# Squares by halves at one stage entrance, a later branch on TensorE, and warm-up products

## The reference

```python
# first block, each layer l
x = x + mixer(rms_norm(x, ...))            # l = 0: pooling, l = 1: latent attention
x = x + hier_moe(rms_norm(x, ffn_norm[l]), ...)   # 32 experts, 2 per token
# between the blocks
x = rms_norm(x, final_norm)
# second block, each layer l
h = swiglu(_rmsnorm(x, g[0]), w_in[l, 0], w_out[l, 0])   # stage "ffn00" for l = 0
x = x + 0.5 * _rmsnorm(h, g[1])
...
```

## Time and profile before

| | us |
|---|---|
| median of 3 runs | 2067.85 (2067.81 to 2069.82) |
| profiled execution | 2067.81 |
| its span, from the first to the last instruction | 2066.0 |
| TensorE busy | 1941.6 (94%) |
| VectorE, ScalarE, GpSimd busy | 877.4, 671.9, 60.4 |
| HBM read | 595.86 MB, 289 GB/s over the span |

### The profile page before, as it was taken

One profiled execution on the slowest core, in us unless ns is written; L12 is line 12 of the kernel. 1 busy time (PEld: TensorE's weight loads), 2 busy tenths in 40 slices (PEclk: granted clock), 3 DMA queues, 4 the chain that ended last, 5 costly groups with the idle time before them and its releaser, 6 DMA issues. The chain is left out here.

```text
span 2066.0 us, 36371 instructions
## 1 busy us (share of the span) xinstructions
PE 1941.6 (94%) x16078; PEld 1376.6 (67%) x16078; DVE 877.4 (42%) x1393; ACT 671.9 (33%) x1138; POOL 60.4 (3%) x97
## 2 busy tenths in 40 slices
PE   6999888988999999999989999999999999999998
PEld 6444344445875444444458888878888888887887
DVE  4011111104651111111156656876665665786663
ACT  2000000003440000000054546664545554676552
POOL 0000000000000000000020000010000000011000
PEclk8999999999999999999999999999999999999999
DMA  9999999998769999999976555336555555425551
GB/s 386 426 426 427 426 427 425 428 424 358 268 244 402 426 428 426 427 425 427 425 288 222 187 180 184 123 116 231 186 181 191 203 190 184 147 100 192 192 195 62
DMA packets 57340, 599.42 MB, mean 290 GB/s; under 512 B 6608, under 2 KB 7120, under 8 KB 10320
## 3 DMA queue, kind: packets, MB, share of 16 engines
q1 hardware_dynamic: 56016, 593.52, 71.9%
q10 hardware_dynamic: 1152, 3.41, 0.6%
HBM read 595.86 MB, written 1.05 MB: 289 GB/s over the span
## 5 line engine op out<-in xcount | busy, mean ns | idle before, releaser
L1972 DVE TENSOR_TENSOR SPLIT<-RING,SPLIT 128x2048 fp32r<-128x2048 f32 (+2 forms) x178 | 398.8, 2256 | 143.1 <-ACT SPLIT L1450 142.8
L752 PE MATMUL PS<-RING,WK 128*32 128x512 f32 x816 | 368.0, 605 | 45.6 <-DVE WK L2236 23.6
L1119 PE MATMUL PS<-HTB,SPLIT 128*128 128x512 f32 x1152 | 404.4, 397 | 0.0
L1450 ACT ACTIVATE SPLIT<-RING 128x2048 fp32r<-128x2048 f32 (+2 forms) x178 | 332.7, 1887 | 47.0 <-DMA RING<-in_units 47.0
L1120 PE MATMUL PS<-HTB,SPLIT 128*128 128x256 f32 x1152 | 321.4, 279 | 0.0
L752 PEld LDWEIGHTS PS<-RING,WK 128*32 128x32 f32 x816 | 86.9, 111 | 289.2 <-issue 253.2
L1119 PEld LDWEIGHTS PS<-HTB,SPLIT 128*128 128x128 f32 x1152 | 216.3, 188 | 51.7
L1598 ACT ACTIVATE WK<-PS 128x128 f32<-128x128 f32 x64 | 17.8, 278 | 700.4 <-PE PS L718 695.7
L1120 PEld LDWEIGHTS PS<-HTB,SPLIT 128*128 128x128 f32 x1152 | 217.0, 188 | 0.2
L718 PE MATMUL PS<-RING,WK 128*32 128x128 f32 x5696 | 184.4, 274 | 7.0 <-issue 5.7
L718 PEld LDWEIGHTS PS<-RING,WK 128*32 128x32 f32 x5696 | 160.3, 109 | 31.0 <-issue 27.3
(11 more groups left out here) (335 smaller groups left out, 2328.3 us busy)
## 6 DMA issues: line engine op xcount, KB each, us to landing
RING<-in_units SPq DMA_DIRECT2D x171, 1024.0 KB, 4.8
RING<-in_w_down SPq DMA_DIRECT2D x53, 2048.0 KB, 35.2
RING<-in_w_gate SPq DMA_DIRECT2D x45, 2048.0 KB, 34.4
RING<-in_w_up SPq DMA_DIRECT2D x44, 2048.0 KB, 36.5
WK<-in_w_up SPq DMA_DIRECT2D x17, 2048.0 KB, 37.8
WK<-in_w_gate SPq DMA_DIRECT2D x16, 2048.0 KB, 36.0
WK<-in_w_down SPq DMA_DIRECT2D x6, 2048.0 KB, 35.2
SEAT<-in_w_up SPq DMA_DIRECT2D x3, 2048.0 KB, 27.8
```

Source lines behind the costliest of these rows:

```text
L752: t = pe.matmul(PS[32 * i:32 * i + 32, 4 + h, :], mo.HE[:, pb, 32 * f:32 * f + 32], v[:, c, 512 * h:512 * h + 512], start=f == 0, stop=f == 3)
L1119: pe.matmul(out.rearrange("p (z b n) -> p z b n", z=2, b=2), wh, HTB[:, :, :, c, :], start=start, stop=False)
L1450: ac.activation(unit_part(u, 0), loaded(u), ACT.Copy).then_inc(s_hi, 1)
L1972: dv.tensor_tensor(unit_part(u, 1), loaded(u), unit_part(u, 0).bitcast(F32), ALU.subtract).then_inc(s_lo, 1)
```

## The change

1. **Squares by halves at the entrance to `ffn00`.** ScalarE squares a half row of 512 columns at a time, of `X` as well as of the gained row, and GpSimd adds up four partial sums instead of two. VectorE makes the gained row in two halves, each with its own semaphore count.
2. **Order at the entrance.** On VectorE the gained row of block 1 moves from ahead of `enter` to behind the low half of u0+1. On ScalarE the high half of u0+1 moves from behind the squares of block 0 to behind the eight `halves` of block 0.
3. **TensorE's branch.** In `moe0` it moves from ahead of step 27 to ahead of step 31. In `moe1` it moves behind step 32 and the last combine, and only the overflow path is left in it, so nothing is written twice there.
4. **Warm-up products.** In both expert layers three go ahead of the `up` products of expert 31, and three behind its turn, ahead of the down products of expert 30.

```diff
-            if n in (2,) or n >= 5:
-                return (4 if n == 2 else 12 + 4 * (n - 5)) + 2 * b + h + 1
-            return {0: 0, 1: 2, 3: 8, 4: 10}[n] + b + 1
+            if n == 2 or n >= 4:
+                return (4 if n == 2 else 10 + 4 * (n - 4)) + 2 * b + h + 1
+            return {0: 0, 1: 2, 3: 8}[n] + b + 1
...
                 part = SM[:, 8 + b:9 + b]
+                po.wait_ge(s_sq, squared(4, b, 0))
+                po.tensor_scalar(part, SM[:, b:b + 1], EPS, EPS * EPS, ALU.mult, ALU.add).then_inc(own.up(), 1)
                 po.wait_ge(s_sq, squared(4, b))
-                po.tensor_scalar(part, SM[:, b:b + 1], EPS / 1024, EPS * EPS, ALU.mult, ALU.add).then_inc(own.up(), 1)
-                po.wait_ge(s_fsq, b + 1)
                 po.wait_ge(own.sem, own.n)
-                po.tensor_tensor(part, part, SM[:, 10 + b:11 + b], ALU.add).then_inc(own.up(), 1)
+                po.tensor_scalar(part, SM[:, 24 + b:25 + b], EPS, part, ALU.mult, ALU.add).then_inc(own.up(), 1)
+                po.wait_ge(s_fsq, 2 * b + 2)
+                po.wait_ge(own.sem, own.n)
+                po.tensor_scalar(part, SM[:, 10 + b:11 + b], SM[:, 14 + b:15 + b], part, ALU.add, ALU.add).then_inc(own.up(), 1)
...
                 for z, name in enumerate(("gate", "up")):
+                    if z and e == 31:
+
+                        keep_warm(pe, 2, 3)
                     pe.wait_ge(*landed((name, l, e)))
...
                         turn_hidden(e)
+                        keep_warm(pe, 2, 3)
                     down(e - 1)
...
-            early = 27
+            early = 31 if l == 0 else 33
 
             def end():
                 for e in range(early, 33):
                     step(e)
-                combine(7)
+                if l == 0:
+                    combine(7)
             for e in range(early):
...
+            if l:
+                combine(7)
             with pe.If(over > 0):
                 end()
                 pe_overflow(pe, l)
-            with pe.Else():
-                end()
+            if l == 0:
+                with pe.Else():
+                    end()
...
                 def gained(b):
-                    ac.wait_ge(s_fg, b + 1)
-                    square(XS[:, b, :], SM[:, 10 + b:11 + b], (s_fsq, b + 1), scale=1 / 32)
+                    for h in range(2):
+                        ac.wait_ge(s_fg, 2 * b + h + 1)
+                        square(XS[:, b, 512 * h:512 * h + 512], SM[:, 10 + 4 * h + b:11 + 4 * h + b], (s_fsq, 2 * b + h + 1),
+                               JK[:, 512 * h:512 * h + 512], 1 / 32)
...
                 gained(0)
-                hi(u0 + 1)
                 scale(0)
                 squares(n, 1)
                 halves(stage, 0)
+                hi(u0 + 1)
                 gained(1)
...
                 lo(u0 + 1)
+                gained(1)
                 scale(1)
...
-                    if l:
-                        gained(1)
...
-                dv.tensor_tensor(XS[:, b, :], X[:, b, :], RB[:, 2, :], ALU.mult).then_inc(s_fg, 1)
+                for h in range(2):
+                    c = 512 * h
+                    dv.tensor_tensor(XS[:, b, c:c + 512], X[:, b, c:c + 512], RB[:, 2, c:c + 512], ALU.mult).then_inc(s_fg, 1)
```

More of the change, by code:

```diff
@@ L568, in pool_program @@
             for b in range(2):
-                inverse_rms(SM[:, 12 + b:13 + b], SM[:, b:b + 1], 1024, (s_sq, squared(4, b)), 1.0, s_frs)
+                inverse_rms_of_halves(SM[:, 12 + b:13 + b], (SM[:, b:b + 1], SM[:, 24 + b:25 + b]), 1.0, (s_sq, squared(4, b)),
+                                      s_frs)
             po.wait_ge(s_x, 8)
@@ L1462, in squares @@
             def squares(n, b):
-                if n in (0, 1, 3, 4):
+                if n in (0, 1, 3):
                     x_ready(n, b)
@@ L1470, in squares @@
                     else:
-                        ac.wait_ge(*((s_cx, 29 + b) if n == 2 else (s_xh, 2 * (n - 5) + b + 1)))
+                        ac.wait_ge(*((s_cx, (29 if n == 2 else 59) + b) if n in (2, 4) else (s_xh, 2 * (n - 5) + b + 1)))
                     square(X[:, b, 512 * h:512 * h + 512], SM[:, b + 24 * h:b + 24 * h + 1],
@@ L2038, in scale @@
                 def scale(b):
-                    dv.wait_ge(s_fg, b + 1)
+                    dv.wait_ge(s_fg, 2 * b + 2)
                     dv.wait_ge(s_rs, 2 * n + b + 1)
```

## The result

The changed kernel took 2080.76 us (median of 4 runs, 2076.13 to 2082.2) beside 2068.84 us of the kernel before (4 runs, 2067.81 to 2070.18): ratio 1.0054, 95% interval 1.0042 to 1.0066, so about 11 us slower. All 21 runs of it on record lie between 2076.1 and 2084.5, with a median of 2080.3. The direction was forecast, the size not: 2080.8 lies outside the range of 2069.3 to 2076.3. The profiled execution took 2079.38 us, with a span of 2077.5.

The account below looks back on a forecast made before the run. With TensorE busy 94% of the span, only its idle stretches, at the expert layers' ends and the handover, could matter. Terms 0 + 0 + 4.8 + 0.6 = +5.4 us on about 2067.8 gave 2073.3 us, range 2069.3 to 2076.3.

Parts of the forecast that it names:

- The bound of the stretches: Last weight slabs decide both expert layers' ends; in the handover to `ffn00` TensorE waits for the vector side.
- one for wrong: Sign against the forecast: u0+2 starts before 1074 us, or a stretch outside the handover moves by over 1.5 us.
- Part 1: Warm-up products at expert 31, both layers: slab waits and ScalarE cover them, 0; 1.2 us lost without layer 1's cover.
- Part 2: TensorE's moved branch: fetch gaps hidden, 0; up to 1.3 us in layer 0, at most 0.5 in layer 1.
- the rule alone: Taken branch forces a fetch; 1.0 us sticks out behind layer 1's combine, giving 2074.3 us; set aside as hidden.
- the rows on who is awaited: Trace rows at the handover where TensorE waits for the vector side; taken to hide the branch's fetch, so 0.
- Part 3: Entrance to `ffn00`: moved squares and high half delay u0+1 by 1.6 us and u0+2 by +4.8 us, the term.
- the clock: Handover: idle ahead of u0+2 may drop TensorE to 1.2 GHz, 4 in 10; +0.6 us, ends 0 and 1.7.
- (a): Rival, slower: layer 0's fetch gap (1.3) and the clock fall (1.7) come on top; 2075.7 us, chance 0.12.
- (b): Rival, no change: ScalarE and VectorE catch up at the handover, +0.9 to +4, about 2070.5 us; chance 0.24.
- (c): Rival, faster: expert layer ends decide, last down quarters no longer wait for DMA; -4.9, 2063 us; chance 0.06.

Follow-up runs that it names:

- e2: Kernel before with only the warm-up trios at expert 31 of both layers; 2068.5 us, ratio 0.9998.
- e14: Kernel before with TensorE's branch moved in layer 0 only, plus both trios in both layers; 2075.5 us, ratio 1.0022.
- e16: Changed kernel without any warm-up trios; 2075.4 us, ratio 1.0028.
- e18: Changed kernel with the warm-up trios in layer 1 only; 2076.7 us, ratio 1.0036.
- e1: Kernel before with only TensorE's branch moved, in both layers; 2071.0 us, ratio 1.0014.
- e11: Changed kernel with TensorE's branch left out in both layers; 2074.5 us, ratio 1.0023.
- e4: Kernel before with TensorE's branch moved in layer 0 only; 2071.4 us, ratio 1.0008.
- e13: Changed kernel without the trio ahead of `up` 31, the trio behind the turn kept; 2080.8 us, ratio 1.0058.
- e15: Kernel before with TensorE's branch moved in layer 1 only, plus both trios in both layers; 2072.6 us, ratio 1.0010.
- e9: Kernel before with the changed entrance and TensorE's branch moved in layer 1 only; 2075.3 us, ratio 1.0028.
- e5: Kernel before with TensorE's branch moved in layer 1 only; 2071.4 us, ratio 1.0011.
- e8: Kernel before with the branch moved in both layers and the trios, entrance as before; 2077.7 us, ratio 1.0037.
- e3: Kernel before with only the entrance changed (squares by halves, new order on ScalarE and VectorE); 2074.2 us, ratio 1.0028.
- e10: e3 with the gained row of block 1 back ahead of the entrance on VectorE; 2069.8 us, ratio 1.0007.
- e17: Changed kernel with only the trio ahead of `up` 31, in both layers; 2076.3 us, ratio 1.0031.
- e12: Kernel before with trios, whole-row squares and another entrance order, block 1's gained row behind the low half of u0+2; 2067.3 us, ratio 0.9985.
- e6: Changed kernel with TensorE's branches where they were before (new entrance and trios only); 2074.5 us, ratio 1.0028.

## Why the prediction was wrong in size

**The bound of the stretches.** Right for the kernel before, and the reason of the error. "At both ends of the expert layers the last slab of weights decides" was used as if it were fixed. The slack it leaves in layer 0 was 1.16 and 0.36 us, plus 1.14 us at 490.96, ahead of the down products, that the text did not count: 2.7 us together. The two gaps of the changed kernel (1.62 and 3.23 us) and its two trios (4.2) come to 9.1, so 6.4 would stick out by this estimate; 5.7 did. Of the signs that the text gave, one for wrong came true, a stretch outside the handover that moves by over 1.5 us.

**Part 1, warm-up products: 0.** Right by themselves (e2). The text named the cover of the first trio, the wait of 1.16 us for the slab of `up` 31, and priced its loss at 1.2 us. It did not ask whether Part 2 takes that cover away. It does: both trios lie on the path in layer 0, the first one at half clock in the profiled execution, behind the gap, and cost some 4 to 5 us there (e14, e16, e18).

**Part 2, the branch: 0, at most 1.3 in layer 0.** This is the step that failed. Both moved branches cost 2.1 us alone (e1, interval 1.0 to 4.8), and 6 to 7 us together with the trios (e11 against the changed kernel). Four things were off. The gap was 3.23 us, not 2.54 (2.06 to 3.64 in the kernels that have it). Of 2.54 us the text let 1.3 reach the end; with the waits that it names it is 1.0, and with the 1.14 us it left out nothing, which is what e16 shows for a single gap of 2.77. A second gap by issue, of 1.62 us (up to 2.17 in others), now falls 14 us ahead of it in seven of the ten profiled executions with this branch (e4, e13 and e16 lack it), where in the kernel before the last gap, at 430 us, left 67 us to catch up with the slabs. The estimate stopped at the gap: in six of these ten the granted clock is at 0.50 right behind it, and what stands next runs at half speed. And in layer 1 the overlap was wrong. The text let the fetch begin at about 1054.4, with the combine, and end 4.7 us behind the combine's start. In all eleven kernels with that branch the packet of q8 starts only 3.8 to 4.0 us behind it (in e13 and e15 the first of two at 3.6 and 3.4), and TensorE restarts at 6.3 to 6.6 us, in e13 and e15 at 7.9 and 7.8. The Trainium skill (Runtime: NRT & Kernel Launch, Instruction fetch mechanics) says that a taken branch outside what is held forces a fetch; the trace agrees (2.67 to 2.88 us of "issue" behind the last combine with a packet of q8 in it, gone in e11). By the rule alone I had 2074.3, and gave it away to the rows on who is awaited. In the handover the rows on who is awaited were right all the same when the clock held (e1, e9: handover as without the branch, because u0+1 is awaited longer) and wrong when it fell (e5, +1.8 us; e8, +3.2).

**Part 3, the entrance: +4.8, and the clock: +0.6.** Right in its mechanism and, within a microsecond, in its size. Alone it measured +5.3 us (e3), and what decides is what the text named, the gained row of block 1 and its squares ahead of the high half of u0+2 (e10). By the traces u0+2 starts 4.05 us later in e3 and 3.5 in e11 (21.06 less 17.57), so the term was mis-sized by about 1 us: u0+1 came 1.2 us later, not 1.6, and the gained row in halves took 1.29 us, not 1.4. GpSimd's power took 0.56 us as taken, and the scale came 0.2 us sooner behind the combine, as forecast (0.25). A unit takes 3.0 us by the text's own rows (3.5 less 0.46), not 2.7, so its idle time ahead of u0+2 would be 3.6 us and not 3.9; nothing hangs on it. The clock was worth more where it fell: in e3, in its slowest execution, u0+2 runs its first eight products cold, some 1.6 us, against the 0.6 that I counted as a mean; in e11 it did not fall on u0+1 or u0+2.

**The rivals.** (a), the gap and the clock on top of the entrance, was the nearest, with half the size: it added 1.3 and 1.7 us, 3.0 in all, where the changed kernel took 6.5 more than e11. It had no trios in it, and they are the larger part. (b) is what e10 shows, a milder entrance; it was not this kernel. (c) did not happen: the last quarter of the down products no longer waits for a DMA in layer 0, as its condition says, but because TensorE is late and not because the slabs came early.

**What stays open.** e13 and e17 together: the trio behind the turn costs 4.5 us by the times (changed kernel 2080.8, e17 2076.3), the other one nothing (e13, 2080.8). By the rows it should be 1.4 and 2.8. The ratios of e13 (1.0045 to 1.0072) and e17 (1.0020 to 1.0042) don't overlap, so the scatter of the runs hardly explains it. Leaving a trio out also moves the place of the gap (in e17 it opens inside the trio, and the clock holds), and no run separates the two; it isn't settled. Nor is it known what decides, in a given execution, whether the clock falls behind the gap.

## What to carry to other kernels

A price of 0 that rests on a wait holds only as long as no other part of the same change uses that wait up: add the parts that share one cover and compare the sum with it. An instruction fetch that falls early in a stretch paced by DMA is made up for; moved to the end of the stretch, the same fetch can be paid, and what follows it may run at the lower clock, work meant to keep the clock up included. When work is moved out of the way at a stage's entrance, it must go behind what the bottleneck engine waits for on that list, not ahead of it: e12, which has that order and whole-row squares, took -2.0 us where e3 took +5.3.

## What the runs showed of the hardware that was not expected

- The gap by "issue" at the branch behind the last combine was 2.67 to 2.88 us in eight profiled executions of kernels with it, 4.09 and 4.25 in two (e15, e13), where two packets of q8 run side by side, and 1.03 in one (e17, where the combine itself ran cold and ended late).
- A gap of 2.7 to 2.9 us there is followed by full clock in some executions (e1, e9: ten warm-up records in 2.43 us) and by half clock in others (3.78 us in e5, 4.63 in e8, 3.97 in the changed kernel). A combine of 3.67 us took 5.25 to 5.91 us in e3, e5, e6, e9, e15 and e17 by such a fall, with no gap by "issue" right ahead of it. One profile is one draw of it.
- Gaps by "issue" of 1.6 to 2.4 us also stand in the middle of gate and up products where no branch is (415.68 us in the changed kernel, 70 us ahead of its branch, and 475.72 in e11, which has none). Where a branch stands ahead, the place of the gap shifts with the code: the six trio products in the side that isn't taken (12 records) bring it 12 records nearer to the branch, with 68 instead of 56 records of the pair of gate and up left behind it (in layer 0, e2, e6, e12 and e15 against before, e3, e5, e9 and e10).
